# Latent norms ahead of the index scores, and relu in place in PSUM

## What is computed

```
(q_lat, c_kv, k_rope, z_a, q_b, k_b, v_b, z_b,
 q_idx, k_idx, w_idx, gate_a, gate_b) = split(h @ w_in)
q  = rmsnorm(q_lat, g_q_lat) @ w_uq          # 384 wide
kv = rmsnorm(c_kv, g_kv_lat) @ w_ukv         # 256 wide
k_pe = rope(k_rope, pos)
# index scores, 8 heads of 32, block of 128 queries
s     = q_idx . k_idx * 32 ** -0.5
score = sum over heads of relu(s) * w_idx * 8 ** -0.5
score = where(key chunk <= query chunk, score, -inf)
idx   = top_k(score, 128)                    # keys that the DSA attention sees
y_a = mla_attention(q_nope, q_pe, k_nope, k_pe, v_a, pos) * silu(z_a)
```

## Time and profile before

| | |
|---|---|
| runs | 1592.29 us median of 3 (1587.42 to 1595.55) |
| profiled execution | 1595.8 us, of this span 1594.0 us |
| TensorE busy | 1489.4 us, 93% |
| VectorE busy | 1055.6 us, 66% |
| GpSimd busy | 846.6 us, 53% |
| ScalarE busy | 467.8 us, 29% |
| chain that ended last | 76% TensorE, 15% DVE, 4% issue, 3% ACT |

### The profile page before, as it was taken

One profiled execution on the slowest core, in us unless ns is written; L12 is line 12 of the kernel. 1 busy time (PEld: TensorE's weight loads), 2 busy tenths in 40 slices (PEclk: granted clock), 3 DMA queues, 4 the chain that ended last, 5 costly groups with the idle time before them and its releaser, 6 DMA issues.

```text
span 1594.0 us, 20010 instructions
## 1 busy us (share of the span) xinstructions
PE 1489.4 (93%) x6946; PEld 1166.6 (73%) x6946; DVE 1055.6 (66%) x1916; ACT 467.8 (29%) x891; POOL 846.6 (53%) x681
## 2 busy tenths in 40 slices
PE   4989999989999999999999999999978999999996
PEld 3877787756777788687888888887756776766884
DVE  7475978887447722578999994336579797675234
ACT  4453442356313211321011011012343334454111
POOL 3531331433466767366776777676447344433763
PEclk9998999989999999999999999999989999999998
DMA  5210110211232333223333333333233531322331
GB/s 206 80 50 30 40 54 28 55 56 56 96 97 80 105 107 106 66 80 90 95 93 101 98 93 106 102 100 124 80 106 95 106 91 54 106 67 80 118 93 53
DMA packets 37883, 137.10 MB, mean 86 GB/s; under 512 B 4264, under 2 KB 4520, under 8 KB 37160
## 3 DMA queue, kind: packets, MB, share of 16 engines
q1 hardware_dynamic: 32976, 120.08, 25.0%
q10 hardware_dynamic: 4824, 15.89, 3.5%
HBM read 129.13 MB, written 6.82 MB: 85 GB/s over the span
## 4 chain that ended last, share of the span: by engine, by line
PE 76%; DVE 15%; issue 4%; ACT 3%; POOL 1%; PEld 0%; DMA 0%; PEldq 0%; DVEq 0%; ACTq 0%; POOLq 0%
PE pair L551 21%; PE pair L553 20%; PE pair L552 20%; PE pair L793 3%; PE pair L821 3%; PE pair L647 2%; PE pair L805 2%; PE pair L648 2%; DVE nL L1576 1%; DVE selm L2082 1%; DVE kk L1789 1%; PE pair L695 1%; DVE nt L1598 1%; DVE dx L1831 1%; DVE rstd L1594 1%
## 5 line engine op out<-in xcount | busy, mean ns | idle before, releaser
L506 POOL TENSOR_TENSOR wL<-ring,wH 128x1024 fp32r<-128x1024 f32 x225 | 558.5, 2482 | 18.8
L551 PE MATMUL pair<-nH,wH 128*128 128x512 f32 x1064 | 430.8, 405 | 23.8 <-DVE nL L1576 9.0
L503 POOL TENSOR_TENSOR tick<-tick 128x1 f32<-128x1 f32 x225 | 55.7, 247 | 705.2 <-PE pair L553 696.0
L552 PE MATMUL pair<-nL,wH 128*128 128x512 f32 x1064 | 419.3, 394 | 0.0
L553 PE MATMUL pair<-nH,wL 128*128 128x512 f32 x1064 | 418.9, 394 | 0.0
L551 PEld LDWEIGHTS pair<-nH,wH 128*128 128x128 f32 x1064 | 202.4, 190 | 91.2 <-issue 25.8
L504 POOL TENSOR_SCALAR wH<-ring 128x1024 fp32r<-128x1024 f32 x225 | 241.3, 1072 | 0.0
L553 PEld LDWEIGHTS pair<-nH,wL 128*128 128x128 f32 x1064 | 202.5, 190 | 43.7
L552 PEld LDWEIGHTS pair<-nL,wH 128*128 128x128 f32 x1064 | 202.9, 191 | 40.9 <-issue 1.2
L1421 ACT ACTIVATE sgb<-cv 128x512 f32<-128x512 f32 x22 | 14.0, 635 | 208.8 <-DVE cv L1997 208.8
L1710 DVE TENSOR_TENSOR X<-E,qT 128x64 f32<-128x64 f32 x224 | 41.1, 226 | 46.0 <-ACT E L1205 45.9
(11 more groups left out here) (359 smaller groups left out, 2765.2 us busy)
## 6 DMA issues: line engine op xcount, KB each, us to landing
ring<-stream SPq DMA_DIRECT2D x225, 512.0 KB, 3.6
gvec<-gv ACTq DMA_DIRECT2D x1, 2560.0 KB
hT<-xT SPq DMA_DIRECT2D x4, 512.0 KB, 5.5
x_d<-hT ACTq DMA_DIRECT2D x1, 2048.0 KB, 6.3
toep<-gvec ACTq DMA_DIRECT2D x8, 256.0 KB, 3.6
hT<-x_d ACTq DMA_DIRECT2D x1, 2048.0 KB, 8.1
outT<-hT ACTq DMA_DIRECT2D x8, 256.0 KB, 2.6
cD<-const_d ACTq DMA_DIRECT2D x1, 1345.0 KB, 6.0
```

What stands on the lines that cost most here:

```text
L503: pool.tensor_tensor(tick[:, 1:2], tick[:, 0:1], tick[:, 0:1], ALU.add).then_inc(high_done, 1)
L506: pool.tensor_tensor(wL[:, r % SPL, :], ring[:, r, :], wH[:, r % SPL, :].bitcast(F32), ALU.subtract).then_inc(split_done, 1)
L551: mm(out, a[0], b[0], start=first, stop=False)
L552: mm(out, a[0], b[1], start=False, stop=False)
```

## The change

In TensorE's order the norm sum of `q_lat` moves from behind the replications to between `q_idx` 0 and 1, and that of `c_kv` from behind the first index scores to behind `small`. Ahead of each set of index scores but the first TensorE waits for the weighted sums of the set before (`t_acc`) instead of its relu.

On ACT the squares of `q_lat` come ahead of everything else behind `mix2`, the square roots and high parts of both norms follow, and all of it stands ahead of the sigmoid of `z_a` 0. The relu writes to the PSUM banks that it reads; the tile `rl` is gone, and with it ACT's wait for `t_acc`. The store of `x1` moves ahead of the sigmoid of `z_a` 1.

On DVE both norms, the rotation of `kp` and its two masked copies `kpz` stand ahead of the first weighted sums. These read PSUM. The rounds of the top-k search are laid out as 2, 2, 2 and 4, then the rotations of `qp`, then 6, instead of 3, 3, 3, then all rotations, then 7. The rotations use the tile `sq` for their partner product, not `sgb`.

```diff
--- before.py
+++ after.py
@@ -386,7 +386,6 @@
         b0 = top[0]
         kp = place("kp", [P, S])
         ki = place("ki", [P, S])
-        rl = place("rl", [P, 2, 2, S])
         pk = place("pk", [P, S], at=rl0)
         top[0] = b0
         qb = place("qb", [P, 4, S])
@@ -992,8 +991,11 @@
             rows = slice(0, REL_BUCKETS)
             mm(bank(4)[0:8, :], relb[:, :], c_d("onehot", 0, S)[rows, :], start=True, stop=True)
             mm(bank(5)[0:8, :TOEP - S], relb[:, :], c_d("onehot", S, TOEP)[rows, :], start=True, stop=True).then_inc(gv_done, 1)
-            project("q_idx", 0, 2, n_parts, inputs="mix2")
+            project("q_idx", 0, 1, n_parts, inputs="mix2")
+            norm_sum("q_lat")
+            project("q_idx", 1, 1, n_parts)
             project("small", 0, 1, n_parts)
+            norm_sum("c_kv")
             project("z_a", 0, 1, n_parts)
 
 
@@ -1014,7 +1016,7 @@
                 i, h4 = n // 2 + 1, n % 2
                 w = P * (i + 1)
                 if n:
-                    pe.wait_ge(t_relu, 2 * n)
+                    pe.wait_ge(t_acc, 4 * n)
                 else:
                     pe.wait_ge(rep_out, 3)
                 for g in range(4):
@@ -1022,10 +1024,8 @@
                     last = mm(bank(2 + g)[:, :w], qi[rows, h4, P * i:P * i + P], ki[rows, :w], start=True, stop=True)
                 last.then_inc(t_sc, 1)
 
-            norm_sum("q_lat")
             project("z_a", 1, 1, n_parts)
             index_scores(0)
-            norm_sum("c_kv")
             project("z_a", 2, 1, n_parts)
             index_scores(1)
             project("z_a", 3, 1, n_parts)
@@ -1035,7 +1035,7 @@
             halves("uq", lambda s: 2 * s, 3, 3, ql, lambda s: index_scores(3 + s))
             pe.wait_ge(nl_made, SPLIT["c_kv"] + 2)
             halves("ukv_k", lambda s: 2 * s, 2, 2, ck)
-            pe.wait_ge(t_relu, 12)
+            pe.wait_ge(t_acc, 3 * IDX_HEADS)
             for c in range(2):
                 rotate("second", 1 + c, qp[:, c, :], FIRST["uq"] + 4 + c, c_d("perm", 0, P))
 
@@ -1445,14 +1445,19 @@
 
 
             highs("mix2", nH, DC)
-            for c in range(2):
-                copy_out("q_idx", c, qi[:, c, :])
+            squares("q_lat", qlat, lambda c: out_of_bank(act, FIRST["q_lat"] + c))
             act.wait_ge(gv_done, 1)
             A(gv[:, :S], bank(4)[0:8, :], ACT.Copy).then_inc(gv_out, 1)
             A(gv[:, S:], bank(5)[0:8, :TOEP - S], ACT.Copy).then_inc(gv_out, 1)
             act.wait_ge(gv_out, 2)
-            squares("q_lat", qlat, lambda c: out_of_bank(act, FIRST["q_lat"] + c))
+            copy_out("q_idx", 0, qi[:, 0, :])
+            deviation("q_lat")
+            squares("c_kv", ckv, lambda c: out_of_bank(act, FIRST["c_kv"] + c))
+            copy_out("q_idx", 1, qi[:, 1, :])
+            highs("q_lat", qlH, 3)
             copy_out("small", 0, pk[:, :])
+            deviation("c_kv")
+            highs("c_kv", ckH, 2)
             sigmoids("z_a", [0])
             act.wait_ge(rep_done, 1)
             A(wtok[:, :, :], bank(4).rearrange("p (t k) -> p t k", k=P)[:, :, 64:64 + IDX_HEADS], ACT.Copy,
@@ -1460,27 +1465,22 @@
             for n, (b, dst) in enumerate(((2, ki), (3, kp))):
                 act.wait_ge(rep_done, 2 + n)
                 A(dst[:, :], bank(b), ACT.Copy).then_inc(rep_out, 1)
+            act.wait_ge(x1_made, DC)
+            act.dma_start(x1_d, hT[:, :, :]).then_inc(st_x1, 16)
 
             def index_relu(n):
+
+
                 w = P * (n // 2 + 2)
                 act.wait_ge(t_sc, n + 1)
-                for m in (2 * n, 2 * n + 1):
-                    if m >= 2:
-                        act.wait_ge(t_acc, 2 * (m - 1))
-                    A(rl[:, m % 2, :, :w], pair[1 + m % 2][:, :].rearrange("p (b t) -> p b t", b=2)[:, :, :w],
-                      ACT.Relu, scale=IDX_SCALE).then_inc(t_relu, 1)
-
-            deviation("q_lat")
+                for half in range(2):
+                    two = pair[1 + half][:, :].rearrange("p (b t) -> p b t", b=2)[:, :, :w]
+                    A(two, two, ACT.Relu, scale=IDX_SCALE).then_inc(t_relu, 1)
+
             sigmoids("z_a", [1])
-            squares("c_kv", ckv, lambda c: out_of_bank(act, FIRST["c_kv"] + c))
             index_relu(0)
-            highs("q_lat", qlH, 3)
-            act.wait_ge(x1_made, DC)
-            act.dma_start(x1_d, hT[:, :, :]).then_inc(st_x1, 16)
-            deviation("c_kv")
             sigmoids("z_a", [2])
             index_relu(1)
-            highs("c_kv", ckH, 2)
             sigmoids("z_a", [3])
             index_relu(2)
             for s in range(3):
@@ -1625,11 +1625,12 @@
                 if m:
                     dve.wait_ge(rotated, m)
                 partners, read = (bank(4 + m % 2 if to is None else to), rot_used) if at is None else (bank(at % 2), freed[at % 2])
-                V.tensor_tensor(sgb[:, m % 2, :], partners, sin, ALU.mult).then_inc(read, 1)
+                part = (sq if name == "second" else sgb)[:, m % 2, :]
+                V.tensor_tensor(part, partners, sin, ALU.mult).then_inc(read, 1)
                 own(V.tensor_tensor(x, x, cos, ALU.mult))
                 if at is not None:
                     out_of_bank(dve, at)
-                V.tensor_tensor(x, x, sgb[:, m % 2, :], ALU.add).then_inc(rotated, 1)
+                V.tensor_tensor(x, x, part, ALU.add).then_inc(rotated, 1)
 
             def residual(stage, name, chunks=range(DC), after=lambda c: None):
 
@@ -2049,17 +2050,25 @@
             low("mix2", DC - 1, nH, nL)
             for c in range(2):
                 scaled("c_kv", c, ckv)
+            accumulate_all("q_lat")
             inverse("mix2")
             for c in range(DC):
                 V.scalar_tensor_tensor(out=hT[:, c, :], in0=hT[:, c, :], scalar=vcol("final_norm", c), in1=rstd[:, :],
                                        op0=ALU.mult, op1=ALU.mult).then_inc(x1_made, 1)
+            dve.wait_ge(x1_made, DC)
+            inverse("q_lat")
+            accumulate_all("c_kv")
+            norm("q_lat", qlat, "g_q_lat_2", qlH, qlL)
+            inverse("c_kv")
+            norm("c_kv", ckv, "g_kv_lat_2", ckH, ckL)
+            silu("z_a", [0], za)
             dve.wait_ge(ld_d, 32)
-            accumulate_all("q_lat")
-            silu("z_a", [0], za)
-            inverse("q_lat")
-            norm("q_lat", qlat, "g_q_lat_2", qlH, qlL)
+            dve.wait_ge(rep_out, 3)
+            rotate("second", 0, kp[:, :], c_d("cos", 0, S), c_d("sin", 0, S), to=6)
+            dve.wait_ge(rotated, ROTATE["second"] + 1)
+            for g in range(2):
+                V.tensor_scalar(kpz[:, g, :], kp[:, :], c_d("parity", g, g + 1), None, ALU.mult).then_inc(kpz_made, 1)
             silu("z_a", [1], za)
-            accumulate_all("c_kv")
             at = {1: 0, 2: 2 * P, 3: 5 * P}
 
             def top_keys(i, rnd):
@@ -2079,33 +2088,25 @@
                     dve.wait_ge(t_relu, 2 * n + k // 2 + 1)
                     if h:
                         dve.wait_ge(t_acc, done)
-                    V.scalar_tensor_tensor(out=acc, in0=rl[:, k // 2, k % 2, :w], scalar=wtok[:, i, h:h + 1],
+                    V.scalar_tensor_tensor(out=acc, in0=bank(2 + k)[:, :w], scalar=wtok[:, i, h:h + 1],
                                            in1=acc if h else c_d("causal", S - w, S),
                                            op0=ALU.mult, op1=ALU.add).then_inc(t_acc, 1)
 
-            dve.wait_ge(rep_out, 1)
             index_sum(0)
-            inverse("c_kv")
             silu("z_a", [2], za)
             index_sum(1)
-            norm("c_kv", ckv, "g_kv_lat_2", ckH, ckL)
             silu("z_a", [3], za)
             index_sum(2)
             dve.wait_ge(t_acc, 8)
             for n in (3, 4, 5):
-                for r in range(3 * n - 9, 3 * n - 6):
+                for r in (2 * n - 6, 2 * n - 5):
                     top_keys(1, r)
                 index_sum(n)
-            for c in (2, 3):
-                out_of_bank(dve, FIRST["z_a"] + c)
-            dve.wait_ge(rep_out, 3)
-            rotate("second", 0, kp[:, :], c_d("cos", 0, S), c_d("sin", 0, S), to=6)
-            dve.wait_ge(rotated, ROTATE["second"] + 1)
-            for g in range(2):
-                V.tensor_scalar(kpz[:, g, :], kp[:, :], c_d("parity", g, g + 1), None, ALU.mult).then_inc(kpz_made, 1)
+            for r in range(6, 10):
+                top_keys(1, r)
             for c in range(2):
                 rotate("second", 1 + c, qp[:, c, :], c_d("cos", 0, S), c_d("sin", 0, S))
-            for r in range(9, TOPK // 8):
+            for r in range(10, TOPK // 8):
                 top_keys(1, r)
             dve.wait_ge(t_acc, 3 * IDX_HEADS)
             barrier()
```

## The result

The changed kernel takes 1573.76 us in the median of 6 runs (1567.98 to 1580.21), the kernel before 1591.31 us in 6 runs beside it. The ratio over the runs is 0.9903, with a 95% interval of 0.9879 to 0.9927: faster by 15.4 us, 11.6 to 19.3. The two medians alone give 17.6 us, a ratio of 0.9890, inside that interval. Either way the gain is under 2% and clear of the spread. The profiled execution took 1575.0 us, span 1573.2 us, against 1595.8 and 1594.0. Forecast were 1576.1 us and 16.2 us less.

The account below looks back on a forecast made before the run. TensorE's own queue was taken as the bound. Removing 13.6 us of waits, 5.3 of clock and 0.3, less 3.0 of new waits, gives 16.2 us: from a median of 1592.3 to 1576.1 us, range 1568 to 1586.

Parts of the forecast that it names:

- 13.6 us of waits: TensorE waits removed: 8.2 us at the c_kv norm sum, 2.5 at za, 2.9 at kn.
- 5.3 of clock: TensorE's slow stretches behind the three removed waits go: 2.1, 1.55 and 1.6 us.
- 0.3 were to go: TensorE's 0.3 us wait for the second qp rotation goes.
- 3.0 to come: New TensorE waits: 0.8, 1.6 and 0.4 us at index scores, 0.2 us kept for a weight slot.
- The walk of VectorE's queue: VectorE's operations timed one by one from 1121.0; sums of set 0 end at 1163.9, barrier reached at 1209.7.
- No clock loss behind 1.8 us of idleness: New TensorE waits at index scores, 1.6 us at most, cost no clock; 2 us kept for the range.
- the weighted sum from PSUM: VectorE's 512-column sums take 0.69 us instead of 1.195, saving 3.5 us on seven, beside TensorE.
- rival B: Relu in place slow, or PSUM sums still held; wait returns on TensorE; 13 or 10 us saved; chance 0.09.
- the 2.9 us wait: TensorE at L551 waits for ScalarE's kn, queued behind a relu whose buffer VectorE had not yet summed.
- A: VectorE's queue later than walked through three more held operations; 7.8 us saved, 1584.5 us; chance 0.17.
- C: Short waits at index scores keep TensorE at 1.2 GHz; about 9 us slower, 1601 us; chance 0.03.
- D: VectorE reaches the barrier late enough to eat the gain; about 1587 to 1592 us; chance 0.04.

Follow-up runs that it names:

- The kernel with one round more: Changed kernel with top-k search rounds 3, 3, 3 and 1 instead of 2, 2, 2 and 4; ratio to the kernel before 0.9875.
- held sums: Changed kernel with relu to SBUF as before and sums reading it there; ratio to the kernel before 0.9957, bias products to first MLA matmul 103.3 us.
- ScalarE freed as well: Changed kernel with relu to SBUF in eight buffers, TensorE waiting for relu only; ratio to the kernel before 0.9952, bias products to first MLA matmul 102.8 us.
- the early bank alone: Changed kernel with the scaled copy of c_kv 0 ahead of the last two low parts of mix2 on VectorE; ratio to the kernel before 0.9891.
- with the queue behind it cleared: Changed kernel with c_kv 0 scaled early, kp rotation and kpz late, final-norm multiplications spread out; median 1568.1 us, ratio to the kernel before 0.9861.

## Why the prediction was right

- **The sum.** 13.6 us of waits, 5.3 of clock and 0.3 were to go, 3.0 to come, 16.2 in all. In the part 18.1 went. The three waits went in full, and their slow stretches too. (By whole times it is 15.4 or 17.6 us; the part is the finer measure.) Of the 2 us between, 0.7 are new waits (2.3 instead of 3.0; in the changed kernel `ukv_k` runs through, with no wait for a weight slot). The other 1.3 are a shorter slow stretch behind the old wait at `q_idx` 0, on which I had put nothing: that product took 8.5 us before (1120.56 to 1129.03) and 7.2 after (1120.05 to 1127.23), behind the same wait of 1.85 and 1.84 us. 19.2 - 2.3 + 1.3 = 18.2.
- **The walk of VectorE's queue** came within 2 us at every point: the reciprocal of `c_kv` done at 1149.4 (1149.5 forecast), `silu` of `z_a` 0 at 1154.2 (1155.8), sums of set 0 begun at 1160.4 and ended at 1162.7 (1163.9). Part of this is luck: the holds did not all fall where they were put. The `c_kv` add and one operation of the `c_kv` norm were put down as held and were free; the final-norm multiplications and the `q_lat` norm took 1 us longer each than forecast. The differences cancel in part. The waits stand where they were put, ahead of sets 0, 1 and 5. The one ahead of set 1 goes when the rotation of `kp` moves away. It is not the only thing that sets it: VectorE also stood still for 1.22 and 0.43 us for ScalarE's sigmoid and `kp` in that queue.
- **No clock loss behind 1.8 us of idleness.** It was left out by choice, since a slow stretch stands behind 1.85 us of idleness. Behind the 1.76 us at 1162.72 the next product's matmuls start 0.23 us apart, and the clock of 1160 to 1180 is 1.00. The kernel with one round more shows the same behind its 1.76 us. But this was no safe rule: with relu in place alone, a wait of 1.54 us with one of 1.24 close behind has a slow stretch behind it that costs 2.9 us. The waits differ by little and I don't claim that the size decides.
- **Mis-sized: the weighted sum from PSUM.** I took 0.69 us from L1740. It takes 0.750, the same as free from SBUF. L1740 was no fair sample: its scalar is a constant and it multiplies twice, while the sums take a column of `wtok` and add; which of these makes the difference was not tried. The 120 cycles from PSUM against 58 that the Trainium skill, "VectorE: DVE Perf Modes", section "The TRN2 errata", gives do not show for this instruction: 0.750 against 0.752.
- **Mis-sized: rival B.** I gave 3 us to the case that sums are held all the same. With held sums the part is 7.2 us longer (103.3 against 96.1), and with ScalarE freed as well still 6.7 (102.8), with 2.6 more behind it. I had credited the 2.9 us wait to ScalarE's buffers, and the shorter sums with something "beside TensorE". They are not beside it: through the relu's buffers (6.5 us at `kn`) or through the barrier (8.5 us) the holding of VectorE reached TensorE both times. Held sums with TensorE itself waiting for them, which is what B names, no run shows.
- The rule of the Trainium skill, "SBUF — State Buffer", section "Who interferes with whom", that one SBUF input stays free of GpSimd, held for all 24 sums: none took over 0.752 us, while GpSimd worked on the low parts of weights (L505 of the changed kernel) for 12.1 of the 30.2 us from the first sum to the last.
- Rivals A, C and D did not come. D's mechanism, VectorE last at the barrier, is real: 1.5 us of it with relu in place alone, 8.5 with eight buffers, and a slow stretch behind both (2.9 and 2.6 us).

## What to carry to other kernels

When two engines take two kinds of work in turn, read which instruction the waiting engine's releaser was queued behind, and move the whole chain that stands early on data (here both norms), not the last link. Work on VectorE with both operands in SBUF beside a GpSimd that splits weights took up to 2.77 us here instead of 0.69, and the weighted sums 1.2 to 2.1 us in the mean instead of 0.75; leaving one operand in PSUM saved 13 us of VectorE (28.2 to 14.8, with the norms early) at no cost per instruction. And a wait in front of a queue is only worth removing once the next thing asked for is ready: the early bank alone made the part 1.3 us longer, with the queue behind it cleared 2.4 us shorter. Look behind the end of your measured stretch too: two variants here lose 2.6 to 2.9 us just after it.
